# The last feed-forward in products of 64 partitions, upper and lower into two banks

## The chip, the cores and the metric

The kernel runs on one core of a Trainium2 chip, as one program. The metric is the device time of one execution in microseconds; where several runs of a kernel were made, their median. Lower is better. The engines are PE (TensorE: matrix products into the 8 banks of PSUM), DVE (VectorE), ACT (ScalarE), POOL (GpSimd) and SP (SyncE, which issues most DMAs). A tile has 128 partitions; a bank holds 512 fp32 columns in each.

## What is computed

Two transformer-like blocks run one after the other on 256 tokens of width 1024, the second one beside 256 context tokens. The part that matters here is the very last feed-forward, on the 256 tokens alone, and the norm behind it:

```python
D_FF = 2816
def swiglu(h, w_in, w_out):
    gate, up = jnp.split(h @ w_in, 2, axis=-1)
    return (jax.nn.silu(gate) * up) @ w_out
# end of the last layer
x = x + 0.5 * m_lat[:, 8] * swiglu(modulate(rms_norm_2(x), m_lat[:, 6], m_lat[:, 7]),
                                   ffn_in[l, 1], ffn_out[l, 1])
return rms_norm_2(x, final_gain)
```

`m_lat` is a product of the condition vector with a modulation matrix, cut into nine parts per layer.

## The kernel before

**Layout.** Activations lie feature-major: `x` is [128, 8 chunks, 512 tokens], the first 256 columns of a chunk being the tokens. A weight matrix streams in as tiles of 1 MB ([128, 8 row chunks, 256 columns]) into a ring of three slots; SP issues the DMA of a tile as soon as PE has released the slot (`tile_used`). A tile is used in two *halves* of 128 output columns, m = 0 and 1. `ffn_halves` lists the 68 halves of a feed-forward in the order of the stream: gate 0, gate 1, up 0, up 1, gate 2, gate 3, and so on to up 21 (44 *input halves*, 8 row chunks each), and then 24 *output halves*: for each pair of the 8 output chunks three parts (8, 8 and 6 of the 22 hidden chunks), each for m = 0 and 1.

**Three products per chunk.** Operands are split into a rounded high part and the rest as a rounded low part (type fp32r), so a product of fp32 quality is high x high + high x low + low x high: three matmuls of 128 partitions x 128 columns of weights with 256 tokens (in the other feed-forwards 512). Plain fp32 matmuls exist elsewhere in the kernel.

**Who does what for a half n of the last feed-forward.** PE waits for `w_split` (n + 1), takes a bank (`take_bank` waits until its last use has been freed; banks turn in a fixed order of eight), and runs 3 x 8 matmuls into it. On ACT and DVE the loop over the halves is the order of work. ACT first splits the high part of half n + 3 (`split_high_last`, AHEAD = 3, line 2266; five slots of split weights in unused columns of `ffn_h_hi`/`ffn_h_lo`), then, for a gate, takes the silu of the bank to `ffn_gate` (`sq`; line 2557), and for an up half waits for DVE's product and rounds it into `h_hi` (line 2563). DVE first splits the low part of half n + 3 (`split_low_last`, line 2864, behind ACT's high part), then writes the low part of the last hidden chunk if the half before was an up half (`hidden_low`, line 3360), then, in the first gate and the first up half of the first four groups, one product of the modulation (`modulate`, line 2758), and, for an up half, multiplies the bank with the gate into `ffn_hidden` (`rs`; line 3386). For an output half nothing is read until its last part is summed; then DVE adds the bank, times its modulation, onto `x` (`gated_add`, line 3088), and ACT squares that chunk for the norm.

The first two halves are done together, chunk by chunk, as the normed chunks of x arrive. The sums of squares are matmuls with ones (`sum_squares`, line 1082).

Two helpers recur: `link(ins)` makes the engine wait until `ins` has finished, and `full_bank()` waits until PE has filled the bank that is next in turn. `tok` is 256 here.

Of the kernel before, what the change touches and what calls it, by code (L numbers as in the profile page):

```python
# [25 lines left out]
ALU = mybir.AluOpType  # L26
ACT = mybir.ActivationFunctionType
# [7 lines left out]
KC = D // P  # L35
# [459 lines left out]
def build(nc, ins, out):  # L495
    order = weight_order()
    with ExitStack() as ctx:
# [499 lines left out]
        def _(pe):  # L997
# [557 lines left out]
            def leave(layer):  # L1555
# [26 lines left out]
                for c in range(ADDED, KC):  # L1582
                    sum_squares(c, token_parts(SEQ, layer))

            def ffn(layer, which, tok):
# [394 lines left out]
        def _(act):  # L1980
# [199 lines left out]
            def other_table():  # L2180
                table[0] = None
# [350 lines left out]
            def ffn(layer, which, tok):  # L2532
                halves = halves_of[2 * layer + which]
                b_g, b_p, b_u = tally("gate_ready", FFC), tally("product_ready", FFC), tally("w_used", len(halves) - 1)
                other_table()

                act.wait_ge(sem("normed"), tally.seen["normed"])

# [7 lines left out]
                for n, h in enumerate(halves):  # L2546
                    if layer == 1 and which == 1:
                        for k in range(EARLY if n == 0 else n + AHEAD, min(n + AHEAD + 1, len(halves))):
                            split_high_last(halves, k, b_u)
                    elif n == 0:  # L2550
                        split_high(halves, EARLY, b_u)
                        split_high(halves, EARLY + 1, b_u)
                    elif EARLY + 1 < n + 1 < len(halves):
                        split_high(halves, n + 1, b_u)
                    if h.kind == "gate":
                        bank, free = full_bank()
                        nc.scalar.activation(ffn_gate[:, h.c % 2, 0:tok], bank[:, 0:tok], ACT.Silu).then_inc(sem("gate_ready"), 1)  # L2557
                        act.wait_ge(sem("gate_ready"), b_g + h.c + 1)
                        act.nop().then_inc(free, 1)
                    elif h.kind == "up":  # L2560
                        turns.next()
                        act.wait_ge(sem("product_ready"), b_p + h.c + 1)
                        nc.scalar.activation(ph5["h_hi"][:, h.c, 0:tok], ffn_hidden[:, h.c % 2, 0:tok],  # L2563
                                             ACT.Copy).then_inc(sem("hidden_hi"), 1)
                    else:
                        if h.k0 == 0 and h.m == 0:
                            if h.c == 4:
                                take_sums(next_parts)
                            if h.c == KC - 2:
                                exp_and_ln()  # L2570
                            if h.c == KC - 2 and ends:
                                last_came[KC - 2], last_came["later"], last_came[KC - 1] = turns.next(), turns.next(), turns.next()
                            else:
# [149 lines left out]
        def _(dve):  # L2723
# [628 lines left out]
            def ffn(layer, which, tok):  # L3352
                halves = halves_of[2 * layer + which]
                next_parts = token_parts(tok, (layer, which) != (1, 1))
                ends = ends_by_tokens(layer, which)
                b_g, b_p, b_h = tally("gate_ready", FFC), tally("product_ready", FFC), tally("hidden_hi", FFC)

                def hidden_low(c):
                    dve.wait_ge(sem("hidden_hi"), b_h + c + 1)
# [3 lines left out]
                for n, h in enumerate(halves):  # L3363
# [17 lines left out]
                    if h.kind == "gate":  # L3381
                        turns.next()
                    elif h.kind == "up":
                        bank, free = full_bank()
                        dve.wait_ge(sem("gate_ready"), b_g + h.c + 1)
# [3 lines left out]
                        dve.nop().then_inc(free, 1)  # L3389
                    else:  # L3390
                        if h.k0 == 0 and h.m == 0:
                            if h.c == 4:
                                take_sums(next_parts)
                            if h.c == KC - 2 and ends:
                                last_came[KC - 2], last_came["later"], last_came[KC - 1] = turns.next(), turns.next(), turns.next()
                            else:
                                pair = [turns.next(), turns.next()]
                        if h.k0 + h.nk == FFC and not (ends and h.c >= KC - 2):
# [274 lines left out]
```

## Time and profile before

| | us |
|---|---|
| median of 3 runs (2485.0 to 2492.19) | 2487.99 |
| the profiled execution | 2484.31 |
| its span, first to last instruction | 2482.5 |
| PE busy in the span | 2331.7 |
| DVE busy | 1495.7 |
| ACT busy | 960.6 |

The profiled execution is one run; the profiler's records give start and length of each instruction, what it wrote and read, and what ended the idle time before it. The span is a little shorter than the execution's own time. Matmul records have a modelled end that includes the drain of the array, so the pace of PE is read from start to start or from a count in a stretch, not from the length of one record. Line numbers (L1676) are those of the kernel before; a tile that is reused keeps the name it was given, so the split weights of this part appear as `ffn_h_hi`/`ffn_h_lo`, the gate as `sq`, the hidden product as `rs`.

### The profile page before, as it was taken

The page shows a single profiled execution, that of the slowest core. Times are in us where ns is not written, and L with a number is a line of the kernel's source. Part 1 is how long each engine was busy: PE and PEld are TensorE (multiplying, and loading weights), DVE is VectorE, ACT ScalarE, POOL GpSimd, SP SyncE. Part 2 cuts the span into 40 slices and gives each one's busy share as a digit, 9 for nine tenths or more (in the row PEclk, how much of TensorE's full clock was granted, in tenths as well). Part 3 has the DMA queues.
Part 4 walks back from the last instruction along what each step waited for, and adds up shares of the span by engine and source line. Part 5 has one row for each costly group of instructions (what it writes and reads, how often), then busy time and mean ns, then how long its engine had stood idle before and what let it go on. Part 6 is the DMA issues. An engine that isn't in the chain of part 4 may idle for free.

```text
span 2482.5 us, 43863 instructions
## 1 busy us (share of the span) xinstructions
PE 2331.7 (94%) x18452; PEld 1970.8 (79%) x18452; DVE 1495.7 (60%) x2463; ACT 960.6 (39%) x1638; POOL 76.5 (3%) x148
## 2 busy tenths in 40 slices
PE   8999999999999988887778999999999999999998
PEld 6688779888888766676776888889888887778997
DVE  5647466755568677666456655566654444576654
ACT  2344135632222556543224523222522322455543
POOL 0000000000001000000000000000000000000000
PEclk9999999999999999998989999999999999999999
DMA  8325535344456310000003344445343444213653
GB/s 310 107 85 170 186 102 171 118 142 147 145 186 211 109 65 34 1 4 21 4 4 136 114 142 147 150 169 179 122 146 140 153 153 157 84 35 121 222 186 135
DMA packets 55923, 311.04 MB, mean 125 GB/s; under 512 B 5936, under 2 KB 9392, under 8 KB 28080
## 3 DMA queue, kind: packets, MB, share of 16 engines
q1 hardware_dynamic: 32944, 224.75, 26.3%
q0 software_dynamic: 20736, 75.51, 9.2%
q10 hardware_dynamic: 2048, 7.98, 0.8%
q8 instruction: 147, 2.41, 0.4%
q14 instruction: 48, 0.39, 0.1%
HBM read 307.16 MB, written 1.05 MB: 124 GB/s over the span
## 4 chain that ended last, share of the span: by engine, by line
PE 79%; DVE 12%; ACT 5%; issue 3%; DVEq 0%; DMA 0%; ACTq 0%
PE bank L1676 16%; PE bank L1679 16%; PE bank L1683 16%; PE bank L1521 5%; PE bank L1518 2%; PE bank L1771 2%; PE bank L1489 1%; PE bank L1496 1%; PE bank L1492 1%; PE bank L1306 1%; PE bank L1313 1%; PE bank L1309 1%; PE bank L1382 1%; PE bank L1617 1%; PE bank L1620 1%
## 5 line engine op out<-in xcount | busy, mean ns | idle before, releaser
L2854 DVE TENSOR_TENSOR w_lo<-ring,w_hi 128x1024 fp32r<-128x1024 f32 (+1 forms) x195 | 232.2, 1192 | 375.1 <-ACT w_hi L2258 375.1
L1676 PE MATMUL bank<-ffn_x_hi,w_hi 128*128 128x512 f32 x984 | 383.0, 389 | 0.0
L1679 PE MATMUL bank<-ffn_x_lo,w_hi 128*128 128x512 f32 x984 | 382.8, 389 | 0.0
L1683 PE MATMUL bank<-ffn_x_hi,w_lo 128*128 128x512 f32 x984 | 382.8, 389 | 0.0
L2258 ACT ACTIVATE w_hi<-ring 128x1024 fp32r<-128x1024 f32 (+1 forms) x195 | 200.2, 1028 | 260.7 <-PE bank L1679 230.0
L2758 DVE SCALAR_TENSOR_TENSOR ms<-mod_rows,c_silu 128x1024 f32<-128x1024 f32 x216 | 263.5, 1220 | 1.9
L1676 PEld LDWEIGHTS bank<-ffn_x_hi,w_hi 128*128 128x128 f32 x984 | 184.7, 188 | 39.0 <-DVE w_lo L2854 0.6
L1683 PEld LDWEIGHTS bank<-ffn_x_hi,w_lo 128*128 128x128 f32 x984 | 184.7, 188 | 38.4
L1679 PEld LDWEIGHTS bank<-ffn_x_lo,w_hi 128*128 128x128 f32 x984 | 184.7, 188 | 37.9
L1676 PE MATMUL bank<-ffn_h_hi,w_hi 128*128 128x512 f32 x484 | 189.1, 391 | 0.0
L1683 PE MATMUL bank<-ffn_h_hi,w_lo 128*128 128x512 f32 x484 | 188.3, 389 | 0.0
L1679 PE MATMUL bank<-ffn_h_lo,w_hi 128*128 128x512 f32 x484 | 188.3, 389 | 0.0
L1521 PE MATMUL bank<-hn,ring 128*128 128x256 f32 x768 | 175.9, 383 | 3.6 <-PE bank L1521 3.3
L2563 ACT ACTIVATE ffn_h_hi<-rs 128x512 fp32r<-128x512 f32 (+1 forms) x88 | 51.0, 579 | 316.9 <-DVE rs L3386 316.9
L1521 PEld LDWEIGHTS bank<-hn,ring 128*128 128x128 f32 x768 | 144.2, 192 | 30.8 <-issue 12.7
L993 POOL DMA_DIRECT2D mod_rows<-in_mod_stream x144 | 76.3, 530 | 2240.4 <-DVEq L2761 1726.2
L2557 ACT ACTIVATE sq<-bank 128x512 f32<-128x512 f32 (+1 forms) x88 | 47.7, 542 | 205.6 <-PE bank L1683 202.9
L2864 DVE TENSOR_TENSOR ffn_h_lo<-ring,ffn_h_hi 128x1024 fp32r<-128x1024 f32 (+1 forms) x68 | 80.5, 1192 | 62.6 <-ACT ffn_h_hi L2266 62.5
L1683 PEld LDWEIGHTS bank<-ffn_h_hi,w_lo 128*128 128x128 f32 x484 | 90.8, 188 | 19.0
L1679 PEld LDWEIGHTS bank<-ffn_h_lo,w_hi 128*128 128x128 f32 x484 | 90.9, 188 | 18.9
L1676 PEld LDWEIGHTS bank<-ffn_h_hi,w_hi 128*128 128x128 f32 x484 | 90.8, 188 | 18.8
L1676 PE MATMUL bank<-ffn_x_hi,ffn_h_hi 128*128 128x256 f32 x336 | 95.1, 283 | 0.0
(542 smaller groups left out, 5155.1 us busy)
## 6 DMA issues: line engine op xcount, KB each, us to landing
ring<-in_stream SPq DMA_DIRECT2D x211, 1024.0 KB, 4.9
mod_rows<-in_mod_stream POOLq DMA_DIRECT2D x144, 512.0 KB, 3.9
one_const<-in_one ACTq DMA_DIRECT2D x1, 1665.0 KB, 14.4
mix_const<-in_two ACTq DMA_DIRECT2D x1, 1440.0 KB, 6.7
win_const<-in_win ACTq DMA_DIRECT2D x1, 1216.0 KB, 5.3
x<-in_x SPq DMA_DIRECT2D x4, 256.0 KB, 4.6
c_silu<-in_c SPq DMA_DIRECT2D x1, 1024.0 KB, 10.0
x<-in_x SPq DMA_DIRECT2D x1, 1024.0 KB, 25.1
```

The lines of the kernel that those rows point to most:

```text
L993: pool.dma_start(mod_rows[:, n % 2, :], ins["mod_stream"][n]).then_inc(sem(f"mod_rows_in{n % 2}"), 16)
L1518: mm = pe.matmul(bank[:, 0:COLS], hn[:, kc, m * P:(m + 1) * P], w[:, kc * COLS:(kc + 1) * COLS], start=kc == 0, stop=kc == KC - 1)
L1521: mm = pe.matmul(bank[:, 0:SEQ], w[:, kc * COLS + m * P:kc * COLS + (m + 1) * P], hn[:, kc, 0:SEQ], start=kc == 0, stop=kc == KC - 1)
L1676: mm = pe.matmul(bank[:, 0:tok], w_high, hi, start=k == 0, stop=False)
L1679: mm = pe.matmul(bank[:, 0:tok], w_high, lo, start=False, stop=False)
L1683: mm = pe.matmul(bank[:, 0:tok], w_low, hi, start=False, stop=last)
L1771: return pe.matmul(part(bank[by_head(c ^ swapped), col]), lhs[r, col], part(rhs[r, col]), start=True, stop=True)
L2258: nc.scalar.activation(place(n)[0][:, 0:h.nk, :], raw_half(h), ACT.Copy).then_inc(sem("w_hi_ready"), 1)
L2563: nc.scalar.activation(ph5["h_hi"][:, h.c, 0:tok], ffn_hidden[:, h.c % 2, 0:tok], ACT.Copy).then_inc(sem("hidden_hi"), 1)
L2758: link(V.scalar_tensor_tensor(products[:].rearrange("p a b -> p (a b)"), mod_rows[:, part // 2, :], 1.0, c_silu[:, part % 2, :], ALU.mult, ...
L2854: V.tensor_tensor(low[:, 0:h.nk, :], raw_half(h), high[:, 0:h.nk, :].bitcast(F32), ALU.subtract).then_inc(sem("w_split"), 1)
L2864: V.tensor_tensor(low[:, 0:h.nk // 2], raw_last(h), high[:, 0:h.nk // 2].bitcast(F32), ALU.subtract).then_inc(sem("w_split"), 1)
```

## The change

Only the last feed-forward, (layer, which) = (1, 1), is touched. On PE each of its 1584 matmuls of 128 partitions becomes two of 64: partitions 0 to 63 of weights and activations into one bank, 64 to 127 into another, alternating. A half takes two banks in place of one; a pair of output halves takes four in place of two. On an input half ACT now copies the first bank to SBUF (to the unused columns 256 to 511 of `ffn_gate` or `ffn_hidden`) and DVE adds the second bank to it; for a gate ACT waits for that sum and takes its silu, for an up half DVE multiplies the sum with the gate. On an output chunk DVE adds the two banks onto `x` one after the other. The sums of squares of this part begin at the last pair of chunks.

```diff
+            def ffn_by_rows(tok):
...
+                def two_banks():
+                    return [take_bank() for _ in range(2)]
...
+                def products(n, kc, to, hi, lo, begins, ends):
+
+                    w_high, w_low = (t[:, kc // 2, kc % 2, :] for t in last_half(n))
+                    for k, (w, part) in enumerate(((w_high, hi), (w_high, lo), (w_low, hi))):
+                        for g, (bank, full) in enumerate(to):
+                            rows = slice(g * C, (g + 1) * C)
+                            mm = pe.matmul(bank[:, 0:tok], w[rows, :], part[rows, :], start=begins and k == 0, stop=ends and k == 2)
+                            if kc == 0 and k == 0 and g == 0:
+                                first(mm)
+                            if kc == 0 and k == 1 and g == 1 and n > 0:
+
+                                mm.then_inc(sem("w_used"), 1)
+                            if ends and k == 2:
+                                mm.then_inc(full, 1)
...
+                    if h.kind != "out":
+                        to = two_banks()
+                        for kc in range(KC):
+                            products(n, kc, to, ph5["x_hi"][:, kc, 0:tok], ph5["x_lo"][:, kc, 0:tok], kc == 0, kc == KC - 1)
+                        continue
+                    if h.k0 == 0 and h.m == 0:
+                        pair = [two_banks(), two_banks()]
+                        if h.c == KC - 2:
+                            sum_squares(0, parts)
...
+                        products(n, kc, pair[h.m], ph5["h_hi"][:, k, 0:tok], ph5["h_lo"][:, k, 0:tok], k == 0, k == FFC - 1)
...
+                if (layer, which) == (1, 1):
+                    return ffn_by_rows(tok)
...
+                def upper_rows(to, tok):
+
+                    bank, free = full_bank()
+                    nc.scalar.activation(to, bank[:, 0:tok], ACT.Copy).then_inc(free, 1)
+                    wait_read(free)
+                    act.nop().then_inc(sem("rows_copied"), 1)
+                    turns.next()
...
+                    if h.kind == "gate" and by_rows:
+                        upper_rows(ffn_gate[:, h.c % 2, SEQ:TOK], tok)
+                        act.wait_ge(sem("gate_summed"), h.c + 1)
+                        nc.scalar.activation(ffn_gate[:, h.c % 2, 0:tok], ffn_gate[:, h.c % 2, SEQ:TOK],
+                                             ACT.Silu).then_inc(sem("gate_ready"), 1)
...
+                        if by_rows:
+                            upper_rows(ffn_hidden[:, h.c % 2, SEQ:TOK], tok)
...
+                def lower_rows(to, n, tok):
+
+                    turns.next()
+                    bank, free = full_bank()
+                    dve.wait_ge(sem("rows_copied"), n + 1)
+                    link(V.tensor_tensor(to, to, bank[:, 0:tok], ALU.add))
+                    dve.nop().then_inc(free, 1)
...
+                    if h.kind == "gate" and by_rows:
+                        lower_rows(ffn_gate[:, h.c % 2, SEQ:TOK], n, tok)
+                        dve.nop().then_inc(sem("gate_summed"), 1)
...
+                    elif h.kind == "up" and by_rows:
+                        lower_rows(ffn_hidden[:, h.c % 2, SEQ:TOK], n, tok)
+                        dve.wait_ge(sem("gate_ready"), b_g + h.c + 1)
+                        V.tensor_tensor(ffn_hidden[:, h.c % 2, 0:tok], ffn_hidden[:, h.c % 2, SEQ:TOK], ffn_gate[:, h.c % 2, 0:tok],
+                                        ALU.mult).then_inc(sem("product_ready"), 1)
...
+                        if h.k0 + h.nk == FFC and by_rows:
+                            cols = slice(0, tok)
+                            for b, use in pair[h.m]:
+                                dve.wait_ge(bank_full[b], use + 1)
+                                link(V.scalar_tensor_tensor(x[:, h.c, cols], psum[b][:, cols], modv[:, layer, 8, h.c, 0:1],
+                                                            x[:, h.c, cols], ALU.mult, ALU.add))
+                                dve.nop().then_inc(bank_free[b], 1)
```

How the rows stand on the engines. ACT, one group of four input halves (gate, gate, up, up) of the kernel before; `ring` to `ffn_h_hi` is the high split of the half three ahead:

```order
L2266 ACTIVATE ffn_h_hi<-ring 128x4x256
L2557 ACTIVATE sq<-bank 128x256
L2266 ACTIVATE ffn_h_hi<-ring 128x4x256
L2557 ACTIVATE sq<-bank 128x256
L2266 ACTIVATE ffn_h_hi<-ring 128x4x256
L2563 ACTIVATE ffn_h_hi<-rs 128x256
L2266 ACTIVATE ffn_h_hi<-ring 128x4x256
L2563 ACTIVATE ffn_h_hi<-rs 128x256
```

The same group on ACT in the changed kernel:

```order
L2330 ACTIVATE ffn_h_hi<-ring 128x4x256
L2605 ACTIVATE sq<-bank 128x256
L2631 ACTIVATE sq<-sq 128x256
L2330 ACTIVATE ffn_h_hi<-ring 128x4x256
L2605 ACTIVATE sq<-bank 128x256
L2631 ACTIVATE sq<-sq 128x256
L2330 ACTIVATE ffn_h_hi<-ring 128x4x256
L2605 ACTIVATE rs<-bank 128x256
L2644 ACTIVATE ffn_h_hi<-rs 128x256
L2330 ACTIVATE ffn_h_hi<-ring 128x4x256
L2605 ACTIVATE rs<-bank 128x256
L2644 ACTIVATE ffn_h_hi<-rs 128x256
```

A copy of a bank has come into each half, and the silu reads SBUF behind it. DVE, the same group before, beginning with the low split in the first gate half; `rs` to `ffn_h_lo` is the low part of a hidden chunk:

```order
L2864 TENSOR_TENSOR ffn_h_lo<-ring,ffn_h_hi 128x4x256
L3360 TENSOR_TENSOR ffn_h_lo<-rs,ffn_h_hi 128x256
L2864 TENSOR_TENSOR ffn_h_lo<-ring,ffn_h_hi 128x4x256 x2
L3386 TENSOR_TENSOR rs<-bank,sq 128x256
L2864 TENSOR_TENSOR ffn_h_lo<-ring,ffn_h_hi 128x4x256
L3360 TENSOR_TENSOR ffn_h_lo<-rs,ffn_h_hi 128x256
L3386 TENSOR_TENSOR rs<-bank,sq 128x256
```

And in the changed kernel:

```order
L2950 TENSOR_TENSOR ffn_h_lo<-ring,ffn_h_hi 128x4x256
L3455 TENSOR_TENSOR ffn_h_lo<-rs,ffn_h_hi 128x256
L3450 TENSOR_TENSOR sq<-sq,bank 128x256
L2950 TENSOR_TENSOR ffn_h_lo<-ring,ffn_h_hi 128x4x256
L3450 TENSOR_TENSOR sq<-sq,bank 128x256
L2950 TENSOR_TENSOR ffn_h_lo<-ring,ffn_h_hi 128x4x256
L3450 TENSOR_TENSOR rs<-rs,bank 128x256
L3484 TENSOR_TENSOR rs<-rs,sq 128x256
L2950 TENSOR_TENSOR ffn_h_lo<-ring,ffn_h_hi 128x4x256
L3455 TENSOR_TENSOR ffn_h_lo<-rs,ffn_h_hi 128x256
L3450 TENSOR_TENSOR rs<-rs,bank 128x256
L3484 TENSOR_TENSOR rs<-rs,sq 128x256
```

An addition (L3450) stands in every half, behind the low split of the half three ahead; in a gate half DVE had nothing of that half's own before. The third place is DVE at a pair of output chunks, before:

```order
L2864 TENSOR_TENSOR ffn_h_lo<-ring,ffn_h_hi 128x4x256 x2
L3088 SCALAR_TENSOR_TENSOR x<-bank,modv,x 128x256
L2864 TENSOR_TENSOR ffn_h_lo<-ring,ffn_h_hi 128x4x256
L3088 SCALAR_TENSOR_TENSOR x<-bank,modv,x 128x256
L2864 TENSOR_TENSOR ffn_h_lo<-ring,ffn_h_hi 128x4x256
```

And in the changed kernel:

```order
L2950 TENSOR_TENSOR ffn_h_lo<-ring,ffn_h_hi 128x4x256 x2
L3510 SCALAR_TENSOR_TENSOR x<-bank,modv,x 128x256 x2
L2950 TENSOR_TENSOR ffn_h_lo<-ring,ffn_h_hi 128x4x256
L3510 SCALAR_TENSOR_TENSOR x<-bank,modv,x 128x256 x2
L2950 TENSOR_TENSOR ffn_h_lo<-ring,ffn_h_hi 128x4x256
```

Each update of `x` has become two, at the same place.

## Rows read from the trace of the kernel before

**Rows 1.** The page: span, and busy us of each engine.

```profile
span 2482.5 us, 43863 instructions
PE 2331.7 (94%) x18452; PEld 1970.8 (79%) x18452; DVE 1495.7 (60%) x2463; ACT 960.6 (39%) x1638; POOL 76.5 (3%) x148
```

**Rows 2.** Busy time by stretch: input halves, output halves. Columns in the first line.

```profile
core 0: us, PE busy (x) PEld busy (x) DVE busy (x) ACT busy (x) POOL busy (x), PEclk, DMA share, GB/s
2284.40:2411.10 126.70, 126.70 (x1058) 126.70 (x1057) 81.70 (x109) 63.56 (x92) 3.17 (x6) 1.00 0.59 203
2411.10:2469.60 58.50, 58.50 (x485) 58.21 (x483) 24.46 (x30) 20.89 (x26) 0.00 (x0) 1.00 0.44 155
```

**Rows 3.** Timeline of ACT, one group: start, length, line, tiles [idle before <-releaser].

```profile
2339.69 1.04 ACT L2266 ACTIVATE ffn_h_hi<-ring 128x1024 fp32r<-128x1024 f32 x1
2341.17 1.06 ACT L2266 ACTIVATE ffn_h_hi<-ring 128x1024 fp32r<-128x1024 f32 x1 [0.17 <-ACT sq L2557]
2342.14 0.36 ACT L2557 ACTIVATE sq<-bank 128x256 f32<-128x256 f32 x1
2342.67 1.06 ACT L2266 ACTIVATE ffn_h_hi<-ring 128x1024 fp32r<-128x1024 f32 x1 [0.17 <-ACT sq L2557]
2345.45 0.42 ACT L2563 ACTIVATE ffn_h_hi<-rs 128x256 fp32r<-128x256 f32 x1 [1.71 <-DVE rs L3386]
2345.77 1.04 ACT L2266 ACTIVATE ffn_h_hi<-ring 128x1024 fp32r<-128x1024 f32 x1
2349.10 1.04 ACT L2266 ACTIVATE ffn_h_hi<-ring 128x1024 fp32r<-128x1024 f32 x1
```

**Rows 4.** Waits, 2284 to 2411 us: total, times, longest.

```profile
ACT ffn_h_hi L2563 <- DVE rs L3386: 48.2, 22, 3.9
ACT sq L2557 <- PE bank L1683: 9.1, 10, 1.3
```

**Rows 5.** Timeline of PE, plain fp32 matmuls: rows alternating, and full.

```profile
881.12 0.70 PE L1441 MATMUL bank<-mix_in_k,mix_in_q 64*128 64x256 f32 x4
...
881.12 1.14 PE L1441 MATMUL bank<-mix_in_k,mix_in_q 64*128 64x256 f32 x8
...
90.05 3.72 PE L1521 MATMUL bank<-hn,ring 128*128 128x256 f32 x16
```

**Rows 6.** Busy time of PE in a stretch of the recurrence: matmuls of 64x64.

```profile
1084.60:1085.90 1.30, 1.15 (x64) 1.00 0.00 0
```

**Rows 7.** Timeline of DVE, the group of rows 3.

```profile
2346.85 1.23 DVE L2864 TENSOR_TENSOR ffn_h_lo<-ring,ffn_h_hi 128x1024 fp32r<-128x1024 f32 x1 [1.44 <-ACT ffn_h_hi L2266]
2347.99 0.42 DVE L3360 TENSOR_TENSOR ffn_h_lo<-rs,ffn_h_hi 128x256 fp32r<-128x256 f32 x1
2348.32 0.42 DVE L3386 TENSOR_TENSOR rs<-bank,sq 128x256 f32<-128x256 f32 x1
```

**Rows 8.** Groups, 2284.4 to 2411 us: xcount, busy us, mean ns, idle before.

```profile
L2864 DVE TENSOR_TENSOR ffn_h_lo<-ring,ffn_h_hi 128x1024 fp32r<-128x1024 f32 x45 | 54.9, 1225 | 45.7 <-ACT ffn_h_hi L2266 45.6
L2266 ACT ACTIVATE ffn_h_hi<-ring 128x1024 fp32r<-128x1024 f32 x45 | 47.3, 1052 | 4.5 <-ACT sq L2557 3.9 <-DVE ffn_x_lo L2892 0.5
L2758 DVE SCALAR_TENSOR_TENSOR ms<-mod_rows,c_silu 128x1024 f32<-128x1024 f32 x8 | 9.8, 1219 | 0.0
...
L2557 ACT ACTIVATE sq<-bank 128x256 f32<-128x256 f32 x22 | 8.2, 373 | 9.1 <-PE bank L1683 9.1
```

**Rows 9.** Timeline of DVE: a modulation product and what follows it.

```profile
2301.55 1.22 DVE L2758 SCALAR_TENSOR_TENSOR ms<-mod_rows,c_silu 128x1024 f32<-128x1024 f32 x1
2302.70 0.08 DVE L2758 DVE_READ_ACCUMULATOR ms<-mod_rows,c_silu 128x1 f32 x1
2302.81 0.42 DVE L3386 TENSOR_TENSOR rs<-bank,sq 128x256 f32<-128x256 f32 x1
```

**Rows 10.** Timeline of ACT: the split of the first stage.

```profile
2283.47 1.06 ACT L2266 ACTIVATE ffn_h_hi<-ring 128x1024 fp32r<-128x1024 f32 x1 [0.49 <-DVE ffn_x_lo L2892]
```

**Rows 11.** Timeline of DVE: an update of x.

```profile
2466.67 0.48 DVE L3088 SCALAR_TENSOR_TENSOR x<-bank,modv,x 128x256 f32<-128x256 f32 x1 [7.90 <-PE bank L1683]
```

**Rows 12.** Busy time of PE in the recurrence, with the granted clock.

```profile
1120.00:1160.00 40.00, 28.00 (x1033) 0.84 0.02 4
```

More of the change, by code:

```diff
@@ L2535, in ffn @@
                 other_table()
+                by_rows = (layer, which) == (1, 1)
+                def upper_rows(to, tok):
[4 more added lines that the diff above has]
+                    turns.next()
                 act.wait_ge(sem("normed"), tally.seen["normed"])
@@ L2554, in ffn @@
                         split_high(halves, n + 1, b_u)
-                    if h.kind == "gate":
+                    if h.kind == "gate" and by_rows:
[3 more added lines that the diff above has]
+                                             ACT.Silu).then_inc(sem("gate_ready"), 1)
+                    elif h.kind == "gate":
                         bank, free = full_bank()
@@ L2560, in ffn @@
                     elif h.kind == "up":
-                        turns.next()
+                        if by_rows:
+                            upper_rows(ffn_hidden[:, h.c % 2, SEQ:TOK], tok)
+                        else:
+                            turns.next()
                         act.wait_ge(sem("product_ready"), b_p + h.c + 1)
@@ L2566, in ffn @@
                         if h.k0 == 0 and h.m == 0:
-                            if h.c == 4:
+                            if h.c == 4 and not by_rows:
                                 take_sums(next_parts)
@@ L2572, in ffn @@
                                 last_came[KC - 2], last_came["later"], last_came[KC - 1] = turns.next(), turns.next(), turns.next()
+                            elif by_rows:
+                                four = [turns.next() for _ in range(4)]
+                                pair_of[h.c // 2] = [four[1], four[3]]
+                                if h.c == KC - 2:
+                                    take_sums(next_parts)
                             else:
@@ L3356, in ffn @@
                 b_g, b_p, b_h = tally("gate_ready", FFC), tally("product_ready", FFC), tally("hidden_hi", FFC)
+                by_rows = (layer, which) == (1, 1)
+                def lower_rows(to, n, tok):
+                    turns.next()
+                    bank, free = full_bank()
+                    dve.wait_ge(sem("rows_copied"), n + 1)
+                    link(V.tensor_tensor(to, to, bank[:, 0:tok], ALU.add))
+                    dve.nop().then_inc(free, 1)
                 def hidden_low(c):
@@ L3391, in ffn @@
                         if h.k0 == 0 and h.m == 0:
-                            if h.c == 4:
+                            if h.c == 4 and not by_rows:
                                 take_sums(next_parts)
@@ L3395, in ffn @@
                                 last_came[KC - 2], last_came["later"], last_came[KC - 1] = turns.next(), turns.next(), turns.next()
+                            elif by_rows:
+                                four = [turns.next() for _ in range(4)]
+                                pair = [four[0:2], four[2:4]]
+                                if h.c == KC - 2:
+                                    take_sums(next_parts)
                             else:
                                 pair = [turns.next(), turns.next()]
-                        if h.k0 + h.nk == FFC and not (ends and h.c >= KC - 2):
+                        if h.k0 + h.nk == FFC and by_rows:
[5 more added lines that the diff above has]
+                                dve.nop().then_inc(bank_free[b], 1)
+                        elif h.k0 + h.nk == FFC and not (ends and h.c >= KC - 2):
                             b, use = pair[h.m]
```

32 lines of the change are left out of this document (31 added, 1 removed).

## The prediction, made before the changed kernel ran

> **What bounds the kernel now.** I read the busy table of the page first: PE (TensorE matmul) is busy 94% of the span, every other engine far less [rows 1]. That is an average, so I then read the last feed-forward alone, by stretches. From 2284.4 to 2411.1 us PE is busy 126.70 of 126.70 us with 1058 matmuls on record, and from 2411.1 to 2469.6 us 58.50 of 58.50, both at a granted clock of 1.00, while DVE is busy 81.70 and ACT 63.56 us of the first [rows 2]. The first stretch is the 44 halves of the two input matrices, 24 products of 128x256 each: 1056 products in 126.7 us are 0.120 us per product, 2.88 us per half. The second is the output matrix: 528 products in all, of which 48 fall before 2411.1, since its first two halves are done by then (2284.4 + 44 x 2.88 = 2411.1). So today PE sets the end of this part.
>
> The reader should then see how near the two other engines are. They work on halves in groups of four: two gate halves, two up halves. Before each half n they split the weights of half n+3 (ACT rounds the high part, DVE subtracts for the low part), and they do that work in program order, ahead of the eviction of half n. ACT's starts of the four splits are 2339.69, 2341.17, 2342.67 and 2345.77, and the next group begins at 2349.10 [rows 3]. In this group they were catching up, so these are the shortest stages: 1.48, 1.50, 3.10 and 3.33 us, 9.41 us together, against 4 x 2.88 = 11.52 us of PE. There are only 2.1 us of slack per group, and in steady state ACT spends part of them waiting for PE (10 of 22 gate evictions waited, 9.1 us) [rows 4]. The 48.2 us that ACT waits for the product of DVE [rows 4] are the inside of that loop: an up stage is a chain that goes from ACT to DVE and back.
>
> **What the change does to PE.** Each of the 1584 products becomes two matmuls of 64 partitions, in different row halves of the array and different banks. The rounded (fp32r) form with 64 partitions doesn't occur in this trace. The nearest rows are plain fp32 with 64x256, rows alternating: four of them take 0.70 us, eight take 1.14 us, so two pairs more cost 0.44 us, 0.22 us per pair; sixteen plain fp32 products of 128x256 take 3.72 us, some 0.22 us each once the last one's drain is taken off [rows 5]. Two 64-row matmuls thus run side by side in the time of one full product. Issue doesn't limit it either: 64 small matmuls of other tiles start within about 1 us, some 0.02 us each [rows 6], and a pair has 0.12 us. [...] Bounds for a pair: 0.108 (it goes) to 0.133 us (twice); I take 0.120, since in the plain rows the pair cost what the product cost.
>
> The Trainium skill ("TensorE: Matmul & The Clock Gate", Part 3, on what overlaps) says that a weight load overlaps with running matmuls only where the row groups differ, which would speak for this change. The trace contradicts it as a rule for this kernel: with all 128 rows in use, loads and matmuls are both recorded as busy for all of 126.70 us [rows 2], so the loads already lie under matmuls. By the rule the pair would take the 0.108 us of my lower bound; that is the third rival.
>
> **What it does to ACT and DVE, on the input halves.** An eviction becomes: ACT copies one bank to SBUF, DVE adds the other bank, and for a gate half ACT then takes the silu of the sum. Each engine's order is unchanged otherwise, so DVE's add stands behind its low split of half n+3, and ACT's silu stands behind that add, and ACT's next split (of n+4) behind the silu. A gate stage, which had no round trip at all, now has one. From the rows, a hop between the two engines is 0.04 us (ACT's split ends 2346.81, DVE starts 2346.85) and the next independent operation on an engine starts 0.09 before the last one's end [rows 3, 7]:
>
> - second gate stage: split 1.05 + hop 0.04 + low split 1.23 - 0.09 + add 0.42 + hop with two semaphore steps 0.13 + silu 0.41 - 0.09 = 3.10 us. The add is priced as the product from a bank (0.42), the silu from SBUF between the one from a bank (0.36) and the copy of the hidden part (0.42); ACT's copy from the bank, some 0.37, lies under DVE's low split [rows 3, 7, 8].
> - first gate stage: the same with the low part of the last hidden chunk ahead of the add, 0.42 - 0.09: 3.43 us.
> - up stages: as before, with an add ahead of the product, and the product must wait for it: 0.42 and some 0.1. The first was 3.01 without its short wait for PE, the second 3.33, now 3.52 and 3.84 us.
>
> Together 13.89 us for a group, where PE needs 11.52. From this point PE isn't the bound on the input halves: its lead of three halves is used up in the first groups, and it then waits for w_split of half n+3 every time. Added to that are the modulation products of DVE (8 in the stretch, 1.22 us, 1.26 from start to next start [rows 8, 9]): today they fit into slack, in the new order they stand between low split and add, on the chain, some 1.3 us each.
>
> The sum: 11 groups x 13.89 = 152.8, and 8 x 1.3 = 10.4, 163.2 us. ACT starts the first stage's split at 2283.47 [rows 10], so the last stage ends at 2446.7, and the split in it that frees PE for half 46 (the third output half) is done 1.5 us before that, at 2445.2. PE begins that half at 2411.1 now. That is **34.1 us later**.
>
> **On the output halves** a stage has only splits, 1.23 us on DVE against 2.2 to 2.9 us of PE, so PE is the bound again: 480 pairs at 0.120 are what they are now. With the pair at 0.108 it is 5.8 us less, at 0.133 it is 6.2 more. Each chunk's update of x becomes two dependent ones of 0.48 us [rows 11]; all but the last lie under PE's next half, and the last adds 0.5 us to the tail.
>
> Sum: 34.1 + 0.5 = 34.6 us. The profiled execution took 2484.31 us (span 2482.5), so it would take 2518.9. The median of the runs shown is 3.7 us above the profiled one: 2522.6, and I say **2522 us**.
>
> **The rivals.**
>
> 1. *The halves don't run side by side* (the change doesn't do what it says): rounded operands make the array take all rows, so 1584 x 0.120 = 190 us more; PE is then slower than the loop (5.76 us per half against 3.5), which hides in it. 2488 + 190 = 2678 us. For it: no row has this form. Against it: [rows 5]. 8%.
> 2. *The clock falls*: PE would idle some 0.6 us in each 3.5 us. In the recurrence, PE busy 28.0 of 40 us, the granted clock is 0.84 [rows 12]. If it fell to 0.84 here, a half would take 3.4 us, which the 3.5 us of a stage still cover, so the price is near nothing; only if it stood at the lower of its two levels (1.2 of 2.4 GHz) for the whole of the input halves would each take up to 2 x 2.88 us, 44 x 2.88 = 127 us more than now, 2615 us. 3%.
> 3. *Faster*: each pair takes 0.108 us and the loop still keeps up, because the adds fit where ACT and DVE wait today. Price: 1584 x 0.012 = 19 us less, and 0.5 more at the end, 2469 us. It decides at a group time of 10.4 us on ACT and DVE; the 9.41 they need now would have to grow by less than 1.0. I count 4.5 more, since the round trip of the gates is not in any slack: it stands in program order between two splits. If the loop lands between 10.4 and about 11.5, there is no difference instead. 3% faster, 2% no difference.
>
> **How the numbers follow.** The loop as the new bound: 84%, 2522 us. Its own range: the pair from 0.108 to 0.133 (-6, +6); each of 44 stages uncertain by 0.1 us down (hops shorter, silu 0.36) and 0.15 up (semaphore steps that I don't see): -4.4, +6.6; the median's place, 3 us either way. All ends together are rare, so 2508 to 2538 us, and it leaves out rivals 1 to 3, some 16%. About 0.3% (7.5 us) is what a measurement of this kernel can tell from no change. Faster by more than that 0.03, within it 0.02, slower by more 0.95.
>
> **What the profile of the changed kernel would show.** If I am right: in the input halves the matmuls of a pair start a few ns apart and pairs 0.11 to 0.13 us apart inside a half, but PE stands still some 0.6 us per half, released by DVE's low split; ACT's splits start 3.1, 3.4, 3.5 and 3.8 us apart in a group, with waits of ACT for DVE's add in gate halves that didn't exist; the waits of ACT for a PE bank are gone; the output halves start near 2445 us and take what they took. Wrong: PE idle near nothing and pairs at 0.24 us (rival 1); a granted clock far below 1.00 from 2290 us on (rival 2); ACT still waiting for PE's banks (rival 3). A silu that waits less than the low split would show that I misread the order on DVE.

## The result, and the profile of the changed kernel

| | before | after |
|---|---|---|
| median, us | 2486.49 (4 runs, 2484.85 to 2492.19) | 2528.36 (4 runs, 2524.84 to 2531.92) |
| ratio | | 1.0164, 95% interval 1.0144 to 1.0184 |
| profiled execution, us | 2484.31 | 2531.92 |
| its span, us | 2482.5 | 2530.1 |

The change costs 41.9 us (36 to 46 by the interval); 2522 was forecast, with 2508 to 2538 as the range. The profiled execution is the slowest of the four and shows 47.6 us more than the profiled one of before. Part of that lies ahead of the change, as one row of ACT's timeline tells (start, length, line, tiles, [idle before <-releaser]):

```profile
2292.15 1.06 ACT L2330 ACTIVATE ffn_h_hi<-ring 128x1024 fp32r<-128x1024 f32 x1 [0.49 <-DVE ffn_x_lo L2978]
```

This is the split of the first stage, at 2283.47 before [rows 10]. It comes 8.7 us late, and nothing in the change stands ahead of it on ACT. Over all traces of this study it starts anywhere from 2279.4 to 2295.7, so this is the spread of one execution against another. I therefore compare the **last stretch**, from that row to the end of the span: 2482.5 - 2283.5 = 199.0 us before, 2530.1 - 2292.15 = 238.0 after, **38.9 us more**. It agrees to 0.5 us wherever two kernels below should take the same, and it lies inside the 36 to 46 us of the medians.

**PE.** The timeline inside a half: start, length, and x2 for the two halves of a pair.

```profile
2435.97 0.28 PE L1606 MATMUL bank<-ffn_x_hi,ffn_h_lo 64*128 64x256 f32 x2
2436.09 0.28 PE L1606 MATMUL bank<-ffn_x_hi,ffn_h_hi 64*128 64x256 f32 x2
2436.21 0.28 PE L1606 MATMUL bank<-ffn_x_lo,ffn_h_hi 64*128 64x256 f32 x2
```

Two matmuls in one row, and the next row 0.12 us on: a pair takes the 0.120 us of a full product. The input halves by stretch:

```profile
core 0: us, PE busy (x) PEld busy (x) DVE busy (x) ACT busy (x) POOL busy (x), PEclk, DMA share, GB/s
2292.20:2455.00 162.80, 138.40 (x2126) 130.69 (x2124) 93.02 (x146) 73.08 (x132) 3.18 (x6) 0.99 0.45 158
```

PE was busy for every microsecond of [rows 2]; now it stands still for 24.4 of 162.8 (and its busy time includes the drain of each last matmul), at a clock of 0.99. The waits of the same stretch: engine, line, for whom; us in total, times, longest.

```profile
ACT ffn_h_hi L2644 <- DVE rs L3484: 49.6, 21, 3.2
ACT sq L2631 <- DVEq L3478: 39.9, 22, 3.1
...
PE bank L1606 <- DVE ffn_h_lo L2950: 23.4, 28, 1.7
```

The second row is the new round trip: ACT's silu waits 39.9 us for DVE's add, where its wait for PE was 9.1 us [rows 4], and that wait for PE is gone. The wait for the product is what it was (49.6 for 48.2). PE waits for the low split, not for a bank. One group of four on ACT, with DVE in the second gate stage:

```profile
2373.14 1.04 ACT L2330 ACTIVATE ffn_h_hi<-ring 128x1024 fp32r<-128x1024 f32 x1
...
2376.62 1.04 ACT L2330 ACTIVATE ffn_h_hi<-ring 128x1024 fp32r<-128x1024 f32 x1
2377.57 0.37 ACT L2605 ACTIVATE sq<-bank 128x256 f32<-128x256 f32 x1
2379.44 0.42 ACT L2631 ACTIVATE sq<-sq 128x256 f32<-128x256 f32 x1 [1.50 <-DVEq L3478]
2379.76 1.04 ACT L2330 ACTIVATE ffn_h_hi<-ring 128x1024 fp32r<-128x1024 f32 x1
...
2383.32 1.04 ACT L2330 ACTIVATE ffn_h_hi<-ring 128x1024 fp32r<-128x1024 f32 x1
...
2387.22 1.04 ACT L2330 ACTIVATE ffn_h_hi<-ring 128x1024 fp32r<-128x1024 f32 x1
...
2377.69 1.23 DVE L2950 TENSOR_TENSOR ffn_h_lo<-ring,ffn_h_hi 128x1024 fp32r<-128x1024 f32 x1 [1.58 <-ACT ffn_h_hi L2330]
2378.84 0.42 DVE L3450 TENSOR_TENSOR sq<-sq,bank 128x256 f32<-128x256 f32 x1
```

Follow it round: split at 2376.62, low split 2377.69, add 2378.84, silu 2379.44, next split 2379.76. ACT's copy out of the bank (2377.57) lies beside the low split and costs nothing. Starts are 3.48, 3.14, 3.56 and 3.90 us apart, 14.08 per group.

### The profile page after: what moved, and what is told of

The parts are those of the page before. It is cut to its first block, busy times and chain, and to the rows that moved or that the text cites. A ratio compares the mean times of both kernels' runs of the same rounds, so it can differ in the third digit from the quotient of the medians.

```text
span 2530.1 us, 47229 instructions
## 1 busy us (share of the span) xinstructions
PE 2357.4 (93%) x20036; PEld 1986.3 (79%) x20036; DVE 1516.2 (60%) x2515; ACT 972.7 (38%) x1682; POOL 76.5 (3%) x148
## 4 chain that ended last, share of the span: by engine, by line
PE 74%; DVE 14%; ACT 7%; issue 5%; DVEq 0%; DMA 0%; ACTq 0%; SPq 0%
PE bank L1740 13%; PE bank L1743 13%; PE bank L1747 13%; PE bank L1521 5%; PE bank L1606 3%; PE bank L1518 2%; PE bank L1835 2%; ACT ffn_h_hi L2330 2%; PE bank L1489 1%; PE bank L1496 1%; PE bank L1492 1%; PE bank L1306 1%; PE bank L1313 1%; PE bank L1309 1%; PE bank L1382 1%
## 5 line engine op out<-in xcount | busy, mean ns | idle before, releaser
L1606 PE MATMUL bank<-ffn_x_hi,ffn_h_hi 64*128 64x256 f32 x704 | 104.2, 293 | 23.4 <-DVE ffn_h_lo L2950 23.4
L2635 ACT ACTIVATE sq<-bank 128x512 f32<-128x512 f32 x66 | 39.5, 598 | 194.4 <-PE bank L1747 193.3
## 6 DMA issues: line engine op xcount, KB each, us to landing
one_const<-in_one ACTq DMA_DIRECT2D x1, 1665.0 KB, 13.5
```

What stands on the lines that cost most here:

```text
L1606: mm = pe.matmul(bank[:, 0:tok], w[rows, :], part[rows, :], start=begins and k == 0, stop=ends and k == 2)
```

## The experiments

The two columns at the right are the median with its ratio to before (95% interval), and the last stretch in the kernel's trace. The kernel before had medians of 2487.1 to 2488.0 us beside them. Where one run was made, the ratio is left out.

| kernel | median, us | ratio | last stretch, us |
|---|---|---|---|
| before | 2486.49 | | 199.0 |
| changed | 2528.36 | 1.0164 (1.0144 to 1.0184) | 238.0 |
| e1 full products, two banks | 2524.25 | 1.0146 (1.0126 to 1.0165) | 236.8 |
| e2 pairs, no adds | 2489.89 | 1.0005 (0.9993 to 1.0017) | 201.3 |
| e3 only ups added | 2494.26 | 1.0022 (1.0010 to 1.0034) | 205.5 |
| e4 one stage later | 2492.14 | 1.0018 (1.0003 to 1.0034) | 201.6 |
| e5 not alternating | 2527.10 | 1.0160 (1.0143 to 1.0177) | 238.0 |
| e6 = e4, outputs with full rows | 2481.49 | one run | 200.3 |
| e7 = e2, upper halves only | 2494.60 | one run | 201.7 |
| e8 rotated | 2527.35 | 1.0160 (1.0145 to 1.0175) | (its first split stands elsewhere) |
| e9 all upper first | 2580.51 | one run | 290.2 |
| e10 = e6, no wait ahead | 2489.64 | 1.0011 (1.0000 to 1.0023) | 199.7 |

### The loop or the pairs: e1 and e2

e1 keeps the copy, add and silu of each half and undoes the pairs; e2 keeps the pairs and undoes the adds of the input halves.

```diff
# e1, PE
-                        for g, (bank, full) in enumerate(to):
-                            rows = slice(g * C, (g + 1) * C)
-                            mm = pe.matmul(bank[:, 0:tok], w[rows, :], part[rows, :], ...)
+                        bank, full = to[at % 2]      # at: chunk of the sum
+                        mm = pe.matmul(bank[:, 0:tok], w, part, ...)
# e2, ACT (DVE alike)
-                        upper_rows(ffn_gate[:, h.c % 2, SEQ:TOK], tok)
-                        act.wait_ge(sem("gate_summed"), h.c + 1)
-                        nc.scalar.activation(..., ffn_gate[:, h.c % 2, SEQ:TOK], ACT.Silu)
+                        nc.scalar.activation(..., bank[:, 0:tok], ACT.Silu)
```

> TensorE does full products of 128 rows again, as before the change, but chunk 0, 2, 4.. of the sum goes to one bank and 1, 3, 5.. to the other; copy, add and silu of the changed kernel stay. The output is the whole sum. Theory A (the loop of ACT and DVE on the way out sets the time, the pairs of 64 rows cost nothing): as the changed kernel, 2528 us (2523 to 2533), ACT's splits 14.07 us apart per group of four halves where no modulation products stand. Theory B (the pairs or their loads slow TensorE): as the kernel before, 2486 to 2490 us.

> TensorE does the pairs of 64 rows into two banks, as changed; in the input halves ACT and DVE evict the upper bank straight as before the change and only release the lower one. It leaves the lower 64 of each 128 rows out of the gate and up sums; the output halves add both banks. Theory A: 2487 us (2486 to 2490), the half 0.5 to 2 us of it the second update of x at the end. Theory B: 2520 us or more.

e1 took 2524.25 us and e2 2489.89: the loss stays without the pairs and goes with the adds. The splits of e1, with products of 128 rows on PE:

```profile
2366.33 1.04 ACT L2330 ACTIVATE ffn_h_hi<-ring 128x1024 fp32r<-128x1024 f32 x1
2369.80 1.04 ACT L2330 ACTIVATE ffn_h_hi<-ring 128x1024 fp32r<-128x1024 f32 x1
2372.94 1.04 ACT L2330 ACTIVATE ffn_h_hi<-ring 128x1024 fp32r<-128x1024 f32 x1
2376.50 1.04 ACT L2330 ACTIVATE ffn_h_hi<-ring 128x1024 fp32r<-128x1024 f32 x1
2380.39 1.04 ACT L2330 ACTIVATE ffn_h_hi<-ring 128x1024 fp32r<-128x1024 f32 x1
```

3.47, 3.14, 3.56, 3.89 us: the stages of the changed kernel, though no row half is used. In e2 PE is busy throughout again, at the pace of the pairs:

```profile
2284.00:2407.00 123.00, 123.00 (x2054) 123.00 (x2054) 77.95 (x105) 61.08 (x90) 3.18 (x6) 1.00 0.59 207
```

### Which part of the loop: e3, e4 and e8

The edits of this and the next two sections are shown in their core. e3 leaves the adds of the up halves and takes away those of the gates. e4 keeps everything and only takes the silu (and the rounding of the hidden product) one stage later on ACT:

```diff
# e4, ACT
                         upper_rows(ffn_gate[:, h.c % 2, SEQ:TOK], tok)
-                        act.wait_ge(sem("gate_summed"), h.c + 1)
-                        nc.scalar.activation(... Silu)           # of this half
+                        if n:
+                            one_later(halves[n - 1])             # silu or rounding of the half before
# e8: ACT and DVE evict half n first, then split half n + 3
-                        split_high_last(halves, n + AHEAD, b_u)
                         upper_rows(...); act.wait_ge(sem("gate_summed"), ...); activation(... Silu)
+                        split_high_last(halves, n + AHEAD, b_u)
```

> Pairs as changed; the gate halves are evicted straight from the upper bank as before the change (the lower 64 of each 128 rows are left out of the gate sums), the up halves keep copy and add. Theory A, that what costs is the new round trip of the gate halves: stages 1.48 + 1.50 + 3.56 + 3.90 = 10.44 us per group against 11.52 of TensorE, so only the four groups with modulation products (13.0) are late, by 6 us less the lead: 2488 to 2494 us, I say 2490. Theory C, that every copy and add costs alike: half the loss, 2507 us.

> The changed kernel with all its work and its whole output, but ACT takes the silu (or the rounding of the product) of half n-1 behind its copy of half n, so that it never waits for an add of the same stage. Work per group: ACT some 7, DVE some 8 us, 10.5 with modulation, under 11.52 of TensorE. Theory A (order and round trip, not the amount of work): 2488 us (2486 to 2491), TensorE without gaps in the input halves. Theory C (the added work itself, or the two banks): 2505 us or more.

> The changed kernel with copy, add and silu (product, rounding) of half n ahead of the weight splits of half n+3 on ACT and DVE. Whole output. Theory A (the loop is a cycle add, silu, high split, low split, add; to turn it doesn't open it): stages still 3.14 us for gates, some 3.5 for ups, 14 us per group, 2528 us (2522 to 2535). Rival D (what costs is that the add stands behind the low split in its stage, so that banks and silu come late): 2490 to 2505 us.

e3 took 2494.26 us, 2490 expected, and 6.5 us more than before in the last stretch, 2.2 of which e2 has too. The adds of the 22 up halves alone thus cost some 4 us, and with those of the 22 gate halves the other 32.5 of the 38.9 are gone. These are not fixed prices of a gate and of an up half. With the gates evicted directly, the longer up stages still fit into the slack under PE; once the gates' round trip has used it up, each up stage counts in full. The opposite case, adds in the gates alone, was not run. From the stages an estimate is 3.48 + 3.14 + 3.10 + 3.33 = 13.05 us per group, 1.5 above PE's 11.52 where the changed kernel is 2.6 above it: some three fifths of the loss, where the 32.5 of 38.9 us would be five sixths. The group without modulation measures 10.63 us (splits at 2353.76, 2355.33, 2356.92, 2360.49 and 2364.39) where I had 10.44, against 11.52 of PE.

e4 does all the work of the changed kernel, has its whole output, and gives back 36.4 of the 38.9 us. PE is busy for 122.50 of 122.50 us again, ACT waits for PE's bank, and the silu behind the copy hardly waits (2.0 us in all). Its 2492.14 us are still 1 us above the range that I gave; the 2.5 us left in its last stretch are the subject of the last section of experiments.

```profile
2296.50:2419.00 122.50, 122.50 (x2046) 122.50 (x2045) 94.87 (x146) 77.02 (x132) 3.19 (x6) 1.00 0.58 206
...
2341.37 1.05 ACT L2330 ACTIVATE ffn_h_hi<-ring 128x1024 fp32r<-128x1024 f32 x1
2343.43 0.38 ACT L2605 ACTIVATE sq<-bank 128x256 f32<-128x256 f32 x1 [1.01 <-PE bank L1606]
2343.93 0.42 ACT L2619 ACTIVATE sq<-sq 128x256 f32<-128x256 f32 x1
2344.25 1.04 ACT L2330 ACTIVATE ffn_h_hi<-ring 128x1024 fp32r<-128x1024 f32 x1
```

The stage is 2.88 us, PE's own, with a microsecond of slack. So neither the amount of work on ACT and DVE nor the two banks cost anything in the input halves: the order did. e8 shows what kind of order. With the eviction ahead of the split nothing is gained (2527.35 us), since add, silu, high split, low split is a closed cycle that merely begins elsewhere:

```profile
2384.23 1.04 ACT L2330 ACTIVATE ffn_h_hi<-ring 128x1024 fp32r<-128x1024 f32 x1
2387.70 1.04 ACT L2330 ACTIVATE ffn_h_hi<-ring 128x1024 fp32r<-128x1024 f32 x1
2391.26 1.04 ACT L2330 ACTIVATE ffn_h_hi<-ring 128x1024 fp32r<-128x1024 f32 x1
2394.82 1.04 ACT L2330 ACTIVATE ffn_h_hi<-ring 128x1024 fp32r<-128x1024 f32 x1
2398.32 1.06 ACT L2330 ACTIVATE ffn_h_hi<-ring 128x1024 fp32r<-128x1024 f32 x1
```

The group takes 14.09 us, as expected, but no stage takes the 3.14 us that I expected of the gates: all four lie between 3.47 and 3.56, since the stages are now cut at another place of the cycle.

### How the row halves run: e5, e7 and e9

e5 gives PE three upper matmuls and then three lower ones; e9 all 24 upper of an input half and then its 24 lower; e7 is e2 with the lower ones left out.

```diff
# e5, PE
-                    for k, (w, part) in enumerate(((w_high, hi), (w_high, lo), (w_low, hi))):
-                        for g, (bank, full) in enumerate(to):
+                    for g, (bank, full) in enumerate(to):
+                        for k, (w, part) in enumerate(((w_high, hi), (w_high, lo), (w_low, hi))):
# e9, PE, input halves
+                        for g in range(2):
                             for kc in range(KC):
-                                products(n, kc, to, ...)
+                                products(n, kc, to, ..., (g,))
```

> The changed kernel with the six matmuls of a chunk in another order: three upper, then three lower, instead of alternating. Everything else as changed, whole output. Theory A (a half of the array can start only when the matmul ahead of it in order has started, so only neighbours in order overlap): upper and lower overlap where they meet, twice per chunk, 4 slots of 0.12 us where alternation needs 3. 3.84 us per input half, 15.4 us per group of four (16.6 in the four with modulation, where the loop still rules): inputs some 9 us longer, the 160 chunks of the later output halves 19 us, 2556 us in all (2545 to 2570). Rival: no overlap at all when not alternating, 5.76 us per half: 2670 us. Rival: the order doesn't matter, 2528 us.

> As e2_pairs_no_adds, but in the input halves only the upper matmul of each pair is issued (and 2 of the 24 lower ones, for their semaphores). It leaves the lower 64 of each 128 rows out of gate and up sums. Theory A (a matmul of 64 rows takes what one of 128 takes, and the lower one runs beside it for nothing): still 0.120 us from start to start, 2.88 us per half, time as e2. Rival (the pair carries some price of issue or of two loads): 0.108 to 0.113 us, 2.6 to 2.7 us per half, DVE and ACT then nearly the bound, 8 to 12 us less than e2.

> In e5 the lower matmuls, three places behind the upper ones in program order, still started within 0.01 us of them. Here all 24 upper matmuls of an input half come first, then its 24 lower ones (from the third half on; output halves alternate as changed). Whole output. If TensorE looks any distance ahead for the idle half of the array: 2528 us. If it reaches only a few matmuls ahead (3 to 4, say), the 48 matmuls of a half overlap only around the two changes of side: 40 to 42 slots of 0.12 us, 4.8 to 5.0 us per half where the loop gives 3.5 to 3.8: 42 halves, some 50 us more, 2575 us (2560 to 2600), and the trace shows single matmuls 0.12 us apart.

My theory of e5 fell: the order made no difference, 2527.10 us and a last stretch of 238.0. The output halves, where PE sets the pace, would have lost 19 us. In the trace upper and lower still come together:

```profile
2410.08 0.29 PE L1606 MATMUL bank<-ffn_x_hi,ffn_h_lo 64*128 64x256 f32 x2
2410.20 0.29 PE L1606 MATMUL bank<-ffn_x_hi,ffn_h_hi 64*128 64x256 f32 x2
2410.32 0.29 PE L1606 MATMUL bank<-ffn_x_lo,ffn_h_hi 64*128 64x256 f32 x2
```

The program has x_hi,h_hi; x_lo,h_hi; x_hi,h_lo for the upper rows and then the same three for the lower. Started in that order, no two neighbours that overlap would have the same operands; here each pair has, so a lower matmul started ahead of two upper ones that stand before it. e9 shows how far this reaches. Singles stand 0.12 us apart; then, with three upper matmuls still to come, the first lower one starts at 2412.08, beside the one before them, and two pairs follow where the sides overlap; then singles again:

```profile
2411.95 0.28 PE L1607 MATMUL bank<-ffn_x_lo,ffn_h_hi 64*128 64x256 f32 x1
2412.07 0.28 PE L1607 MATMUL bank<-ffn_x_hi,ffn_h_lo 64*128 64x256 f32 x1
2412.08 0.39 PE L1607 MATMUL bank<-ffn_x_hi,ffn_h_hi 64*128 64x256 f32 x2
2412.30 0.29 PE L1607 MATMUL bank<-ffn_x_lo,ffn_h_hi 64*128 64x256 f32 x2
2412.42 0.29 PE L1607 MATMUL bank<-ffn_x_hi,ffn_h_lo 64*128 64x256 f32 x2
2412.54 0.28 PE L1607 MATMUL bank<-ffn_x_hi,ffn_h_hi 64*128 64x256 f32 x1
```

The next change of side is at 2414.57, 2.50 us on, so 24 matmuls of one side take 20.8 slots of 0.12 us. e9 lost 52 us to the changed kernel in the last stretch, as expected of a reach of 3 to 4. An order set ahead of time, when the program was made, could account for e5, but hardly for sides that overlap by three matmuls and no more. In e7 single matmuls of 64 rows are still 0.12 us apart:

```profile
2350.92 0.28 PE L1609 MATMUL bank<-ffn_x_hi,ffn_h_lo 64*128 64x256 f32 x1
2351.04 0.28 PE L1609 MATMUL bank<-ffn_x_hi,ffn_h_hi 64*128 64x256 f32 x1
```

Its stretch is that of e2 (201.7 for 201.3). So the second of a pair costs nothing, and the first costs what 128 rows do.

### The last 2.6 us: e6 and e10

e2 and e4 are 2.2 and 2.5 us longer than before in the last stretch. PE's timeline near the end of the kernel before, and of the changed one:

```profile
2466.34 0.28 PE L1683 MATMUL bank<-ffn_h_hi,ffn_h_lo 128*128 128x256 f32 x1
2466.47 0.60 PE L1082 MATMUL bank<-sq,base 128*128 128x256 f32 x2
2466.71 0.47 PE L1676 MATMUL bank<-ffn_h_hi 128*128 128x256 f32 x1
2467.02 0.28 PE L1679 MATMUL bank<-ffn_h_lo,ffn_h_hi 128*128 128x256 f32 x1
```

```profile
2512.46 0.28 PE L1606 MATMUL bank<-ffn_h_hi,ffn_h_lo 64*128 64x256 f32 x2
2512.67 0.70 PE L1082 MATMUL bank<-sq,base 128*128 128x256 f32 x2
2513.30 0.38 PE L1606 MATMUL bank<-ffn_h_hi 64*128 64x256 f32 x2
2513.52 0.28 PE L1606 MATMUL bank<-ffn_h_lo,ffn_h_hi 64*128 64x256 f32 x2
```

A sum of squares (two plain matmuls of all rows) between products took 0.37 us from product to product. Between pairs of half rows it takes 0.84. The product after that follows sooner, though, in 0.22 us for 0.31, so that the whole passage takes 1.06 us for 0.68, 0.38 more. There are two such places, not the three that I wrote ahead of e6, so 0.8 us; it is also 0.7 of the 1.1 us by which e1, without half rows, is shorter than the changed kernel. And ahead of the first product stand 18 matmuls that keep PE busy while x is normed; of before, then of after:

```profile
2270.02 5.97 PE L1092 MATMUL bank<-base 128*128 128x384 f32 x18
```

```profile
2280.11 7.61 PE L1092 MATMUL bank<-base 128*128 128x384 f32 x18 [1.25 <-DVEq L2900]
...
2280.70:2284.70 4.00, 4.00 (x10) 2.15 (x9) 3.62 (x8) 3.94 (x8) 0.00 (x0) 0.68 0.01 4
```

The change takes four banks ahead of them in place of two, and one of the new two is still being read: PE waits 1.25 us, and the 4 us from 2280.7 are at a granted clock of 0.68. The products of the first halves therefore begin later. Measured from the split of the first stage, the third half starts 0.84 us later before, and 1.50, 1.50 and 1.46 us later in e2, e4 and e6. There PE is the bound, so that these 0.6 us are in their time.

```diff
# e6 = e4, and on PE for output halves
-                        products(n, kc, pair[h.m], ...)
+                        full_products(n, kc, pair[h.m], ...)     # 128 rows, chunks by turns into the two banks
# e10 = e6, and
-                taken = [two_banks() for _ in range(2)]
+                taken = [two_banks()]
                 keep_busy(taken[0][0][0], WARM)
+                taken.append(two_banks())
```

> As e4_one_stage_later, but the output halves use full products of 128 rows, even chunks of the sum to one bank and odd ones to the other, so that TensorE goes to half arrays and back not at all in the last 60 us. Whole output. In the traces so far the stretch from the first split of this feed-forward to the end is 199.05 us before, 201.6 in e4 and 201.3 in e2. Theory A: 1.4 us of that is TensorE waiting for its own matmuls at each of the three sums of squares (0.84 us where it was 0.37) as it goes from half to full array and back, 0.6 us the second update of x: so 200.2 us here, 0.37 us at each sum of squares. Rival (it is the two banks or the updates of x): 201.5 us.

> As e6_outputs_full_rows, but TensorE takes banks 3 and 4 only behind the 18 matmuls that keep it busy ahead of the first products, and so doesn't wait for them (1.25 us in all kernels with the change, none before; the 18 then took 7.7 instead of 5.97 us, at a granted clock of 0.68). Whole output; all of copy, add, silu and second update stay. Expected: the 18 take 5.97 us again, at 1.00, and the stretch from their start to the end is 212.5 us before, 250.0 in the changed kernel, here 213.0 to 213.3 us. Time 2487 us, no difference from before that can be measured (ratio 0.998 to 1.002). If the wait comes back in another place: 213.6 as e6.

```profile
2274.91 5.97 PE L1092 MATMUL bank<-base 128*128 128x384 f32 x18
```

e6 has 200.3 us (e4: 201.6), and e10 has 199.7: its 18 matmuls take 5.97 us again, the third half starts 0.84 us behind the first split, and from the start of the 18 to the end it takes 213.1 us, where 213.0 to 213.3 were expected. That leaves 0.6 us. Half of it stands behind the last product (13.5 us to the end for 13.2): the second update of x, which adds 0.63 us on DVE (1.11 for 0.48), is half covered there, since the two banks of e10 are not full at the same time. The other half lies among PE's products, and no run explains it. e6's 2481.49 us, lower than any run of before, is one run whose last feed-forward merely begins early (first split at 2279.43); its last stretch is 1.2 us longer.

In the end e10 keeps the pairs, the copy, the add and the silu of every input half and both banks of every half, and takes 1.0011 (1.0000 to 1.0023) of the time before. No version had a shorter last stretch than the kernel before: PE gains nothing from the pairs, so there was nothing to win on its side.

## Why the prediction was right, step by step

- **PE bounds the part, 2.88 us per half.** Shown by e2, where PE is busy throughout.
- **A pair takes what a full product took, 0.120 us.** Measured at 0.12, from bounds of 0.108 and 0.133. The plain fp32 rows [rows 5] carried over to the rounded form. The bounds suppose that 0.012 us of the 0.120 can fall away or be paid twice; no run shows such a part, for pairs, single matmuls of 64 rows (e7) and full products all start 0.12 us apart. By the rule of the Trainium skill ("TensorE: Matmul & The Clock Gate", Part 3) that a weight load overlaps with running matmuls only where the row groups differ, the pair would have been faster. It was not, and e7 shows no gain in time even for half the loads.
- **The loop becomes the bound, 3.43 + 3.10 + 3.52 + 3.84 = 13.89 us.** Measured 3.48, 3.14, 3.56, 3.90, 14.08. Each stage is 0.04 to 0.06 longer. ACT's copy was under cover, as said; the hop from add to silu is 0.18 us (2378.84 + 0.42 to 2379.44) where I had 0.13.
- **Modulation 8 x 1.3 = 10.4 us.** The 44 stages took 165.4 us (2292.15 to 2457.58), 11 x 14.08 = 154.9 of it the groups and 10.5 the rest. The eight stages with a modulation product are some 1.27 us longer, 10.2 us. The rest is small: the first stage, without a hidden chunk to split, is 0.3 us shorter, and two up stages are 0.4 us longer.
- **Half 46 starts 34.1 us later.** It started 127.6 us behind the first split before (2411.1) and 163.9 after (2456.03): 36.3 us, the missing 2.2 being the longer stages, 165.4 for 163.2.
- **Behind the start of half 46, 0.5 us.** Measured 2.6 (38.9 - 36.3). This term was mis-sized, since it holds the second update of x alone. From the last product to the end it is 0.7 us more, 0.63 of it that update. The two sums of squares add 0.8. Half 47 adds 1.0: its high split stands behind the last rounding on ACT, so PE waits once more for a low split (row below), and its first pairs start 1.04 and 0.22 us apart for 0.12 each. The same slow first pair at half 46 adds 0.1.

```profile
2459.93 0.39 PE L1606 MATMUL bank<-ffn_h_hi 64*128 64x256 f32 x2 [0.76 <-DVE ffn_h_lo L2950]
```

- **The order on DVE** (the silu waits for the low split and the add) held, and e4 and e8 show it to be the cause. PE didn't wait for w_split "every time", though: it waited ahead of 28 of the 44 halves, three in each group without modulation.
- **The rivals.** One (no overlap) and three (PE faster) fell with the 0.12 us. Two, the clock: it stayed at 0.99 in the input halves although PE stood still between so many of them. The fall that I had not seen is that ahead of the first product, since I did not ask what the two further banks wait for; in the changed kernel it hid behind PE's lead.

38.9 us against 34.6 is an error of 4.3 us, 2.2 in the stages and 2.1 behind them. The median landed 6.4 us above the forecast; the 2 us between are within the spread of a median, which I had put at 3 us either way.

## What to carry to other kernels

Ask of every wait that is added whether it closes a cycle between two engines: here adds of 0.4 us cost 0.8 us per half (36.4 us in 44), because add, silu, high split and low split followed each other around, and the same work one stage later cost nothing there. Turning the cycle did not open it (e8); moving one member to another turn of the loop did (e4). What such a wait costs also depends on the slack that other waits have left (e3). When a step takes more banks, look at who frees each, and where it is first waited for.

## What the runs showed of the hardware

- Rounded matmuls of 64 rows in the two row halves run side by side: 0.120 us per pair, the time of one alone (e7) and of one of 128 rows [rows 2].
- PE starts them out of program order between the halves: with three of one side ahead nothing was lost (e5), with 24 ahead the overlap was 3.2 slots per change of side (e9, 2.50 us for 24). The Trainium skill ("TensorE: Matmul & The Clock Gate", Part 3) says that matmuls start and end strictly in program order; e5 contradicts that for matmuls in different row halves. All of them depend only on banks and operands that are ready; what happens with a wait for a semaphore in between was not tried.
- Going from half rows to all rows and back costs 0.3 to 0.4 us more than staying with all rows, measured to the second product behind (1.06 us at both places of the changed kernel; 0.68 at both of before, 0.68 and 0.78 in e6, where no half rows stand there).
- A wait of 1.25 us lengthened the 18 matmuls behind it from 5.97 to 7.61 us. The granted clock was 0.68 in the mean of 4 us, so for a part of them it was at the lower of its two levels (1.2 of 2.4 GHz); without the wait (e10) they took 5.97 again. The wait was the second in a row: PE had waited 1.08 us for the last square, with one sum of squares (0.70 us) between, and that first wait alone stands in before (1.09) and e10 too. The gaps of the input halves, up to 1.7 us each but between busy stretches, left the clock at 0.99.
